# Loading two 1024 x 1024 matrices by halves of their rows instead of halves of their columns

## What is computed

```
act = gelu(einsum('thkd,td->thk', u[e], x))        # u[e], v[e]: gathered rows, 128 per token
out = einsum('thk,thkd->td', gates * act, v[e])
```

## Time and profile before

| | |
|---|---|
| time, median of 3 runs | 2259.17 us (2254.94 to 2259.38) |
| profiled execution | 2258.05 us, span 2256.3 us |
| busy over the span | PE 76%, PEld 62%, DVE 54%, ACT 40%, POOL 26% |
| mean granted PE clock | 0.854 |
| DMA | 777.21 MB, 183335 packets, mean 344 GB/s |
| q0 (gather) | 539.80 MB, 74720 packets |
| q1 (SP's loads) | 235.15 MB |
| loads touched | ple_w_gate x8, b_w_out x4, 2048 KB each |

### The profile page before, as it was taken

The page is one execution under the profiler, slowest core; times in us unless marked ns, Lnnn a source line. Parts: engine busy times, 40 slices in busy tenths (PEclk is TensorE's granted clock), DMA queues, the critical chain, the costliest instruction groups (busy, mean ns, idle before and its releaser), DMA issues.

```text
span 2256.3 us, 25092 instructions
## 1 busy us (share of the span) xinstructions
PE 1715.9 (76%) x9720; PEld 1405.1 (62%) x9720; DVE 1216.9 (54%) x3105; ACT 907.2 (40%) x1294; POOL 595.8 (26%) x569
## 2 busy tenths in 40 slices
PE   8998755555767786576778656778877779989998
PEld 6458644445556675455657645468777468868863
DVE  3647687886544559854555896455534255610001
ACT  1113454455544544554455445455654212510000
POOL 1002233444333332333333335543323000000000
PEclk9999876777888797689879867878998888999999
DMA  7639999999999999999999999999999768664350
GB/s 268 244 103 376 415 400 411 400 408 421 386 418 413 416 415 408 405 394 417 413 415 415 397 413 411 409 400 413 410 411 414 274 224 299 235 224 149 112 191 33
DMA packets 183335, 777.21 MB, mean 344 GB/s; under 512 B 11584, under 2 KB 19328, under 8 KB 115888
## 3 DMA queue, kind: packets, MB, share of 16 engines
q0 software_dynamic: 74720, 539.80, 58.4%
q1 hardware_dynamic: 107920, 235.15, 28.3%
q10 hardware_dynamic: 576, 0.66, 0.1%
HBM read 774.52 MB, written 1.05 MB: 344 GB/s over the span
## 4 chain that ended last, share of the span: by engine, by line
PE 43%; DMA 31%; DVE 15%; ACT 5%; POOL 3%; issue 3%; another core or an unknown queue 0%; SPq 0%; DVEq 0%; POOLq 0%; ACTq 0%
PE bank L318 34%; DMA arena<-in_uv,eidx 25%; PE bank L546 9%; DVE arena L1845 5%; DMA ring<-in_peer_w_q 3%; ACT arena L1211 3%; DMA ring<-in_w_in_2r 3%; POOL arena L1196 3%; DVE y_tok L1776 2%; DVE y_tok L1772 1%; ACT L1211 1%; DVE y_tok L1812 1%; DVE y_tok L1813 1%; DVE y_tok L1809 1%; DVE mid_region L1768 0%
## 5 line engine op out<-in xcount | busy, mean ns | idle before, releaser
L546 PE MATMUL bank<-ident,arena 128*128 128x128 f32 x4096 | 663.9, 329 | 421.5 <-ACT arena L1211 421.1
L546 PEld LDWEIGHTS bank<-ident,arena 128*128 128x128 f32 x4096 | 586.3, 171 | 499.4 <-ACT arena L1211 487.9
L1845 DVE CUSTOM_DVE_ANT_0 arena<-arena,x_tok 128x1024 f32<-128x1024 f32 x512 | 621.4, 1224 | 493.7 <-DMA arena<-in_uv,eidx 493.3
L1196 POOL DMA_INDIRECT arena<-in_uv,eidx x512 | 576.3, 1126 | 1139.8 <-PE bank L546 900.8
L1211 ACT ACTIVATE arena<-arena,coef 128x1024 f32<-128x1024 f32 x512 | 559.9, 1141 | 285.2 <-DVE coef L1856 277.0
L318 PE MATMUL bank<-xT,ring 128*128 128x128 f32 (+2 forms) x3104 | 478.0, 317 | 64.7 <-DMA ring<-in_w_in_2r 24.6
L318 PEld LDWEIGHTS bank<-xT,ring 128*128 128x128 f32 (+1 forms) x3104 | 441.5, 202 | 100.2 <-DMA ring<-in_w_in_2r 26.4
L1211 ACT ACTIVATE glu<-dots 128x2 f32<-128x2 f32 x256 | 52.0, 203 | 438.0 <-DVE dots L1845 432.4
L318 PE MATMUL bank<-ring,xT 128*128 128x512 f32 (+3 forms) x384 | 164.2, 583 | 0.0
L1211 ACT ACTIVATE arena<-bank 128x256 f32<-128x256 f32 (+1 forms) x62 | 30.0, 490 | 301.1 <-PE bank L318 295.9
L1211 ACT ACT_TABLE_LOAD x112 | 143.7, 1283 | 2.8 <-PEq L2313 0.8
(11 more groups left out here) (243 smaller groups left out, 1134.0 us busy)
## 6 DMA issues: line engine op xcount, KB each, us to landing
ring<-in_w_in_2r SPq DMA_DIRECT2D x20, 2048.0 KB
ring<-in_peer_w_q SPq DMA_DIRECT2D x16, 2048.0 KB
ring<-in_w_ada SPq DMA_DIRECT2D x12, 2048.0 KB
ring<-in_ple_w_gate SPq DMA_DIRECT2D x8, 2048.0 KB
ring<-in_a_w_in SPq DMA_DIRECT2D x6, 2048.0 KB
ring<-in_w_ffn_gate SPq DMA_DIRECT2D x5, 2048.0 KB
ring<-in_w_ffn_up SPq DMA_DIRECT2D x5, 2048.0 KB
ring<-in_w_ffn_down SPq DMA_DIRECT2D x5, 2048.0 KB
```

The source lines that it names most:

```text
L546: ins = nc.tensor.matmul(bank(f"pe{l}_{tb}_{c // 4}")[:, (c % 4) * P:(c % 4 + 1) * P], gath[:, s, D + c * P:D + (c + 1) * P], ident[:, :], ...
L1196: pool.indirect_dma_start(gath[:, i % SLOTS, :], None, a["uv"], bass.IndirectOffsetOnAxis(ap=eidx[:, tb, i:i + 1], axis=0)).then_inc(sem(f ...
L1845: v.tensor_tensor_reduce(out=gath[:, s, 0:D], in0=gath[:, s, 0:D], in1=xt[:, tb, :], scale=1.0, scalar=0.0, op0=ALU.mult, op1=ALU.add, acc ...
```

## The change

Each matrix comes in two loads of 512 whole rows (k chunks 0 to 3, then 4 to 7) with all 1024 columns. Over the first load PE adds up column half 0 and then half 1, and both sums stay open in their banks; over the second load it adds the rest to half 0 and closes it, then to half 1. The first load's slot is freed by a new semaphore `row_part_used`, at the end of slot "0b". ACT's `gate(0)`, DVE's `product(0)` and DVE's `residual("mix1", tb, 0)` each move one slot later. The number of loads, their bytes, the matmuls and the slots stay.

```diff
--- before.py
+++ after.py
@@ -371,6 +371,26 @@
                 ins = mm(o[:, 0:n], src[:, k, ts], w[:, k, wc], k == 0, k == kc - 1)
             if ks[-1] == kc - 1:
                 close(ins, name)
+
+        row_parts = [0]
+
+        def tok_rows(name, src, w_dram, ts, after):
+            for part in range(2):
+                w, rec = take(w_dram[part * 512:part * 512 + 512, :].rearrange("(k p) n -> p k n", p=P), 4, D)
+                for half in range(2):
+                    nm = f"{name}_{half}"
+                    o = bank(nm) if part else open_(nm)
+                    for k in range(4):
+                        ins = mm(o[:, :], src[:, 4 * part + k, ts], w[:, k, half * 512:half * 512 + 512],
+                                 part == 0 and k == 0, part == 1 and k == 3)
+                    if part:
+                        close(ins, nm)
+                        last_use(rec, nm)
+                    elif half:
+                        row_parts[0] += 1
+                        ins.then_inc(sem("row_part_used"), 1)
+                        rec["done"] = (sem("row_part_used"), row_parts[0])
+                    yield f"{after} {part}{'ab'[half]}"
 
         def transposes(name, src, chunks, tb, ready, n):
             pe.wait_ge(ready, n)
@@ -586,13 +606,7 @@
             last_use(rec, f"pp{l}_{tb}_1")
             yield "move x"
             await_T(f"xP{l}", tb)
-            for half in range(2):
-                w, rec = take(rows(a["ple_w_gate"][l], half * 512, 512), KC, 512)
-                tok(f"pg{l}_{tb}_{half}", xT, w, cols(tb), 512, KC, ks=range(0, 4))
-                yield f"gate {half}a"
-                tok(f"pg{l}_{tb}_{half}", xT, w, cols(tb), 512, KC, ks=range(4, 8))
-                last_use(rec, f"pg{l}_{tb}_{half}")
-                yield f"gate {half}b"
+            yield from tok_rows(f"pg{l}_{tb}", xT, a["ple_w_gate"][l], cols(tb), "gate")
             yield "product"
             yield "add"
 
@@ -720,14 +734,7 @@
         def out_slots(tb):
             for g in range(NA):
                 moved(pe, f"lO_{tb}_{g}")
-            for half in range(2):
-                w, rec = take(rows(a["b_w_out"][0], half * 512, 512), KC, 512)
-                nm = f"mix1_{tb}_{half}"
-                tok(nm, M["oT"], w, slice(0, P), 512, KC, ks=range(0, 4))
-                yield f"out {half}a"
-                tok(nm, M["oT"], w, slice(0, P), 512, KC, ks=range(4, 8))
-                last_use(rec, nm)
-                yield f"out {half}b"
+            yield from tok_rows(f"mix1_{tb}", M["oT"], a["b_w_out"][0], slice(0, P), "out")
             yield "add"
             yield "sqrt"
             yield "apply"
@@ -1316,8 +1323,8 @@
             yield "move x"
             yield "gate 0a"
             yield "gate 0b"
+            yield "gate 1a"
             gate(0)
-            yield "gate 1a"
             yield "gate 1b"
             gate(1)
             yield "product"
@@ -1882,8 +1889,8 @@
             yield "gate 0a"
             yield "gate 0b"
             yield "gate 1a"
+            yield "gate 1b"
             product(0)
-            yield "gate 1b"
             yield "product"
             product(1)
             v.scalar_tensor_tensor(xt[:, tb, :], yt[:, tb, :], 0.5, xt[:, tb, :], ALU.mult, ALU.add
@@ -1966,8 +1973,8 @@
         def out_slots(tb):
             yield "out 0a"
             yield "out 0b"
+            yield "out 1a"
             residual("mix1", tb, 0)
-            yield "out 1a"
             yield "out 1b"
             residual("mix1", tb, 1)
             ln_stats(halves(tb))
```

## The result

The changed kernel takes 2263.8 us (median of 22 runs, 2259.74 to 2268.83), the kernel before 2257.36 us (22 runs, 2252.59 to 2262.96). The ratio is 1.0028 with a 95% interval of 1.0020 to 1.0036: slower by 6.4 us, where 2.5 us of gain were forecast. The time lies in the stated range, but it moved the other way.

A forecast was written before the change was run, and what follows sets the result against it. It took DMA to bound 280 to 1780 us and PE the last 476 us; 2.5 us of DMA gain, with slots and order at 0, made 2258.05 - 2.5 = 2255.6 us, range 2249.0 to 2264.0 us.

The forecast's parts named there:

- Packets: Weight loads on q1: one 4 KB piece replaces two of 2 KB, saving 13.2 ns; 4.6 us over eleven loads.
- Slots and order: PE's quarters, ring slots, banks and later evacuations in gate and output: cost 0.
- lifted waits: ACT's 5.22 us before tanh and DVE's 3.14 us before the residual go; hidden behind PE's quarters, so no gain.
- The value of DMA time: Gather beside and behind eleven weight loads: DMA time saved becomes kernel time, 1.5 to 4.6 us, taken as 2.5 us.
- the prediction's own sum: Per load: 14.41 us landing plus 8.80 us for the gather's other 3.67 MB, 23.21 us against 23.35 before.
- the 8.94 us of breaking even: Time after each shortened load in which the gather must move its other 3.67 MB, at 411 GB/s, to lose nothing.
- the forecast 0.14 us: Gain per weight load if the gather runs at 417 GB/s behind it; 1.5 us for eleven loads.
- bared gather: Rival: the row loop alone behind each load is too slow, losing 0.62 us a load at 384 GB/s; 2264.9 us, chance 0.15.
- threshold of 393 GB/s: Gather-only rate behind the loads below which the kernel would be slower by over 4.5 us.
- the 402 GB/s from 410 us on: Mean gather-only rate with stalls behind the first two gate loads, over 190 us; argued against the slower rival.
- The page's rule: Each DMA engine takes turns between its queues at packet granularity, so the turns seen in the trace are general.
- Bytes only: Rival: the wire is the limit, packet size shifts only who uses it; 2258.1 us or up to 1.5 less, chance 0.3.

The follow-up runs named there:

- e4: The kernel before with only ACT's gate(0), DVE's product(0) and the residual of half 0 one slot later: 2260.2 us, ratio 1.0006.
- e1: The changed kernel with each load of whole rows moved in 2 KB pieces again: 2259.33 us, ratio 1.0007 to the kernel before.
- e8: The changed kernel with SP holding the gate loads until the coming window's expert choice is finished: 2285.69 us, ratio 1.0126 to the kernel before.
- e7: The kernel before with only ple_w_gate by row halves, moved in 1 KB pieces, output as before: 2252.58 us, ratio 0.9986.
- e12: The kernel of e7 run once more, unchanged: 2255.24 us, ratio 0.9996 to the kernel before.
- e10: As e7, but with the gate's pieces at 512 B: 2256.73 us, ratio 1.0000 to the kernel before.

## Why the prediction was wrong

**Packets: right.** The number fell by 6144, the duration went to 158 ns (157.6 forecast), the queues take turns, q1 runs at 148 GB/s and the gather at 272 (145.5 and 269.5 forecast). These hold whether or not they bring time.

**Slots and order: right.** Moved evacuations cost nothing (e4), open sums and the order of quarters cost nothing that can be told from zero (e1). The lifted waits gave nothing that can be told; the rows show PE's two quarters ending next, as forecast.

**The value of DMA time: wrong, and this is the step that failed.** The sum let the gather's other 3.67 MB follow a load at 417 GB/s, or 402, taken from stretches in the first window and its end. In the expert choice of the second and third windows the gather can move only 316 GB/s, even with no load beside it (e8), since DVE takes no more. Put into the prediction's own sum, a load there costs 3.67/0.316 = 11.6 us instead of the 8.94 us of breaking even, 2.7 us more; four such loads are 10.7 us, the other seven at the forecast 0.14 us win 1.0, in sum +9.7 us. The 8.4 us that groups 48 to 56 lost in the two windows are of that size. The measured +6.4 us is somewhat less. Where the rest comes from isn't settled; the profiles of e7 and e12, one and the same kernel, drift apart by over 3 us at some points, so the profiles can't tell.

**What should have been read.** The rival "bared gather" named this mechanism, its threshold of 393 GB/s follows from its rows, and it got a chance of 0.15. That its 2264.9 us lies so near the measured time is partly luck: it put a small loss on all eleven loads, and the runs show a large one on four. The argument against it, the 402 GB/s from 410 us on, came from the first window. There the choice is spread over the whole window (its searches run until 484 us) and leaves DVE time, as the stretch of the first window in which gate loads land shows in the kernel before:

```profile
340.00:400.00 60.00, 28.90 (x148) 26.20 (x146) 43.46 (x137) 24.39 (x31) 23.46 (x20) 0.67 1.02 413
```

DVE is busy 43.46 of 60 us there, so what the gather loses it can make up. In the second and third windows the choice is packed into the last third. The stage means did the rest: DVE busy 922 of 1500 us hides that it is busy 72.66 of 75 us exactly where the loads land. A window over the landing of the touched loads would have shown two full resources at once. There the 323 GB/s that 2 KB pieces leave to the gather meet the 316 to 320 GB/s that DVE can use.

**The page's rule.** The Trainium skill, page "DMA: Bandwidth & Descriptors", section on queues, rings and completion order, lets each DMA engine take turns between queues by packets. The trace agrees where both queues are full (744 to 742), and by it the piece size of one queue is the other's share. On the size of a turn it differs from the page: the page has an engine drain a packet of typically 9 to 17 descriptors before it switches, while one of the profile's packets here is a single piece. In the kernel before, from 347 to 398 us, the counts of the two queues stay within 4 of each other over some 4500 packets on 16 engines, which fits turns of about one piece and hardly turns of nine or more. The rule was cited beforehand as agreeing and not carried to its end. "Bytes only", from the same page's port limit, would have given no change. It is refuted as the whole story, since equal bytes took 6.4 us more.

## What to carry to other kernels

Where two DMA queues are both full, the size of one queue's pieces sets the other's share here (323 GB/s beside 2 KB pieces, 272 beside 4 KB). So look at who waits for the squeezed queue in that stage before making pieces bigger. A share of 1.00 doesn't mean that DMA time saved is time saved; take a window over just the stretch in which the touched transfers land, and see whether an engine is also full there. Filling a compute-bound stage with background loads was worth 22 us here (e8). It is worth most when they take only what is left over.

## What the runs showed beyond that

A piece of half the size cost little: the gate's 8 loads in 1 KB pieces add 8192 packets to q1 (116112 against 107920), and the kernel was not slower for it. Even 512 B pieces stayed at 1.0000. A likely reason is that in the choice stage the DMA has the time; this wasn't tested by itself. Small pieces also keep SP longer at issuing: the two gate loads of the second window take it 0.92 us in the changed kernel, 20.56 us in e7 and 30.89 us in e10. PE waited for no gate matrix in any of the three, so it cost nothing here.
